# Gate groups of a product-key expert layer: 48 blocks with two groups each in place of 64 with one and a half, a column as the comparison's second scalar, and later first row gathers

## What is computed

```python
top_s, top_i = lax.top_k(s, 16)            # per head and half: 16 of 128 sub-keys
expert_idx, gates = ...                    # per token and head: 16 of 128 x 128 experts
def block_fn(args):
    xb, ib, gb = args
    u = jnp.take(expert_u, ib, axis=0)
    act = jax.nn.gelu(jnp.einsum('td,thkd->thk', xb, u).astype(jnp.float32))
    w = (gb * act).astype(xb.dtype)
    v = jnp.take(expert_v, ib, axis=0)
    return jnp.einsum('thk,thkd->td', w, v)
```

## Time and profile before

| | before |
|---|---|
| median of 3 runs | 4706.14 us (4703.5 to 4707.44) |
| the profiled execution: its own time | 4705.2 us |
| the profiled execution: its span | 4703.3 us |
| busy: TensorE, VectorE, ScalarE, GpSimd | 4041.3, 2219.0, 1623.2, 1626.7 us |
| granted TensorE clock, mean of the span | 0.885 |

### The profile page before, as it was taken

How to read it: one execution, slowest core, us unless ns; L and a number is a source line. 1 busy time by engine, 2 the same in 40 slices (tenths; PEclk the granted TensorE clock), 3 DMA queues, 4 the chain that set the end, 5 groups by cost and what they waited for, 6 DMA issues and landing times. The chain is left out here.

```text
span 4703.3 us, 53589 instructions
## 1 busy us (share of the span) xinstructions
PE 4041.3 (86%) x17473; PEld 3196.8 (68%) x17473; DVE 2219.0 (47%) x4053; ACT 1623.2 (35%) x2537; POOL 1626.7 (35%) x896
## 2 busy tenths in 40 slices
PE   6798768998769989998877979696989888889998
PEld 5437556876525458886765857575889888878886
DVE  1642172321233323302483141313788988768887
ACT  2322253322241133312353112322324666533334
POOL 3103234433200024433353422232468555543221
PEclk8759889998865579999988989897999999999999
DMA  2002102222100013222201312121366677899997
GB/s 87 28 8 82 60 19 76 97 91 68 47 15 1 0 48 104 89 80 80 69 1 54 95 52 72 58 85 65 125 214 227 220 260 266 277 360 359 343 344 250
DMA packets 275081, 573.60 MB, mean 122 GB/s; under 512 B 119777, under 2 KB 156001, under 8 KB 274545
## 3 DMA queue, kind: packets, MB, share of 16 engines
q1 hardware_dynamic: 238080, 437.71, 28.3%
q0 software_dynamic: 36864, 134.23, 8.4%
HBM read 517.33 MB, written 54.53 MB: 122 GB/s over the span
## 5 line engine op out<-in xcount | busy, mean ns | idle before, releaser
L382 PE MATMUL ps<-h_hi,w_hi 128*128 128x512 f32 (+1 forms) x3020 | 1155.7, 383 | 276.8 <-POOL w_lo L2158 95.4
L383 PE MATMUL ps<-h_lo,w_hi 128*128 128x512 f32 (+1 forms) x3020 | 1144.2, 379 | 0.0
L384 PE MATMUL ps<-h_hi,w_lo 128*128 128x512 f32 (+1 forms) x3020 | 1142.8, 378 | 0.0
L476 POOL TENSOR_TENSOR w_lo<-ring,w_hi 128x1024 fp32r<-128x1024 f32 (+3 forms) x193 | 463.3, 2401 | 1141.4 <-ACT w_hi L453 1141.4
L382 PEld LDWEIGHTS ps<-h_hi,w_hi 128*128 128x128 f32 x3020 | 585.2, 194 | 378.3 <-issue 146.2
L384 PEld LDWEIGHTS ps<-h_hi,w_lo 128*128 128x128 f32 x3020 | 584.1, 193 | 80.8
L383 PEld LDWEIGHTS ps<-h_lo,w_hi 128*128 128x128 f32 x3020 | 585.3, 194 | 78.4
L453 ACT CAST w_hi<-ring 128x1024 fp32r<-128x1024 f32 (+3 forms) x193 | 202.7, 1050 | 867.6 <-PE ps L384 808.3
L2158 POOL TENSOR_TENSOR w_lo<-ring,w_hi 128x1024 fp32r<-128x1024 f32 x142 | 363.0, 2560 | 336.3 <-ACT w_hi L2033 335.9
L2033 ACT CAST w_hi<-ring 128x1024 fp32r<-128x1024 f32 x270 | 281.9, 1044 | 383.6 <-PE ps L384 294.7
L382 PE MATMUL ps<-w_hi,one_hots 128*128 128x512 f32 x768 | 304.5, 396 | 4.1 <-DVE one_hots L2415 4.1
(11 more groups left out here) (358 smaller groups left out, 6969.6 us busy)
## 6 DMA issues: line engine op xcount, KB each, us to landing
ring<-in_expert_u SPq DMA_DIRECT2D x128, 512.0 KB, 4.1
ring<-in_expert_v SPq DMA_DIRECT2D x128, 512.0 KB, 5.6
ring<-in_w_gate_up SPq DMA_DIRECT2D x88, 512.0 KB, 3.7
acts<-expert_gelu SPq DMA_DIRECT2D x128, 192.0 KB, 1.9
gates<-peer_region SPq DMA_DIRECT2D x48, 512.0 KB, 3.1
peer_region<-acts SPq DMA_DIRECT2D x128, 192.0 KB, 4.6
peer_region<-gates SPq DMA_DIRECT2D x128, 192.0 KB, 5.6
ring<-in_w_down SPq DMA_DIRECT2D x32, 704.0 KB, 4.1
```

Source lines behind the costliest of these rows:

```text
L382: pe.matmul(out, w_hi, x_hi, start=start, stop=False)
L383: pe.matmul(out, w_hi, x_lo, start=False, stop=False)
L384: return pe.matmul(out, w_lo, x_hi, start=False, stop=stop)
L476: pool.tensor_tensor(half(c.w_lo, s), raw(s), half(c.w_hi, s).bitcast(F32), ALU.subtract).then_inc(c.lo_done.sem, 1)
```

## The change

Four edits. (1) `GATED` is 48 and each of these blocks has two groups, 2b and 2b + 1; the 24 blocks behind them are plain (8 before). (2) `rows_by`: the first four gathers stand behind `low` of block 14 in place of 8, the further early ones are spread over the blocks from there to 56, and in the gated blocks there are two gathers behind each `low`. Behind the `low` of block 56 + b the gathers asked so far are 26 + 2b (from b = 3 on); before, 28 + 1.5b rounded down. (3) SyncE stores up to two pieces of the gate table per block, in the plain blocks too, where before it stored one per block and all those left at once behind the last gated block. (4) The comparison L2401 takes a column of ones from SBUF as its second scalar in place of the constant 1.0, as L2402 beside it takes the gate's column.

```diff
-GATED = 64
-TAIL = 4
+GATED = 48
+GATHER_AT = 14
@@
 def groups_of(b):
-    return range((3 * b + 1) // 2, (3 * b + 4) // 2)
+    return range(2 * b, 2 * b + 2)

 def rows_by(n):
-    if n < 8:
+    if n < GATHER_AT:
         return 0
     if n < PLAIN:
-        return 4 + (n - 8) * EARLY_DOTS // (PLAIN - 8)
-    return min(P, 4 + EARLY_DOTS + max(0, (3 * (n - PLAIN - 4) + 6) // 2))
+        return 4 + (n - GATHER_AT) * EARLY_DOTS // (PLAIN - GATHER_AT)
+    return min(P, 4 + EARLY_DOTS + max(0, 2 * (n - PLAIN - 4) + 3))
@@ SyncE
-                    for h, e in waiting[0:1]:
+                    for h, e in waiting[0:2]:
                         keep_gates(h, e)
-                    waiting = waiting[1:]
+                    waiting = waiting[2:]
@@
-                for h, e in waiting:
-                    keep_gates(h, e)
                 for n in range(PLAIN + GATED, LAST):
                     up(n + 4, n % 4)
                     keep_act(n, n % 4)
+                    for h, e in waiting[0:2]:
+                        keep_gates(h, e)
+                    waiting = waiting[2:]
@@ VectorE
-                        dve.tensor_scalar(hots[:, 0, g % 3, s, :], iota[:], IJG[:, 0, t], 1.0, ALU.is_equal, ALU.mult)
+                        dve.tensor_scalar(hots[:, 0, g % 3, s, :], iota[:], IJG[:, 0, t], c.ones[:, 0:1], ALU.is_equal, ALU.mult)
```

## The result

| | before | changed |
|---|---|---|
| median | 4706.79 us (4 runs beside the changed kernel: 4703.5 to 4707.44, and one of 7889.4) | 4904.65 us (4 runs, 4902.18 to 4906.15) |
| profiled execution: own time, span | 4705.2, 4703.3 | 4906.15, 4904.2 |
| granted TensorE clock, mean | 0.885 | 0.868 |

The ratio of the fast runs, which leaves the one of 7889.4 us out, is 1.0422, 95% interval 1.041 to 1.0435: the changed kernel is 4.2% slower. The forecast was 4912 us, between 4862 and 4962.

What follows compares the result with a forecast made beforehand. It took the loop of late-asked rows in the gated blocks as the bound. Stage +224.8 us, first gathers -18, V blocks unchanged: +206.8 on the profiled 4705.2 gave 4912 us, range 4862 to 4962.

Steps and rivals of the forecast that it cites:

- Rows are asked late, and the loop now carries two groups: In the gated blocks, low parts, `high`, `low`, gather, dot and one-hots form a loop, carrying two groups per turn, not three.
- The round: One turn of the loop in the gated blocks, from low parts to low parts: 13.5 us, 44 of them.
- VectorE's wait for rows: VectorE's total wait for gathered rows, claimed to grow from 56 us to about 207 us or more.
- The gather 5.2: Landing time of a gather in the loop, 5.2 us, a little above the median of 5.1 because of stores ahead.
- The stage: From TensorE's arrival at block 56 to the first V block: 511.7 us before, 736.5 after, so +224.8.
- The tail's 3 for transfers: Added for transfers in the plain blocks behind the gated ones: 3 us, bounds 0 and 10.
- the burst of stores: Eight stores at once behind the gated blocks and TensorE's 10.17 us behind them, claimed to be gone after the change.
- The first gathers, 18: First gathers moved from block 8 to block 14: 18 us gained before block 56, between 10.9 and 20.2.
- The column, 0.24 on the loop and no end to the holds: L2401's second column: 0.06 us per start, 0.24 per round; L2401 still held while GpSimd makes `low`.
- (A): Rival: rows no wait, nothing held; gated blocks at VectorE's pace, 6.4 us each; about 4600 us; 4 in 100.
- (B): Rival: rows no wait but holds remain; gated blocks 8.8 us each; no change, 4705 us; 3 in 100.
- (C): Rival: TensorE, its clock falling, joins the loop; round some 15.3 us, +79, about 4990 us; 5 in 100.

## Why the prediction was right

By its own steps:

- *Rows are asked late, and the loop now carries two groups.* Right, and shown: the chain has the predicted links, and moving the gathers by two rows took 214 us away. The round was put at 13.5 and is 13.36 on average. VectorE's wait for rows was put at 207 us and is 204.6.
- *The gather 5.2.* Right as a mean (5.1 over the rounds), of two kinds: 4.1 to 4.6 with no stores and 5.9 to 6.7 with two.
- *The stage.* 736.5 forecast, 728.7 measured. Of the 7.8 us less, 6.5 had come by the last one-hots (622.0 behind the arrival at block 56, forecast 622.9 + 5.6), which is the 0.14 per round. The tail's 3 for transfers was near: one wait of 2.38. The gain that the prediction saw in the burst of stores gone is real with 48 blocks, but what the spread stores saved behind the loop (11.5 us) they cost within it (12.3 from group 5's one-hots to the last).
- *The first gathers, 18.* The changed kernel's profile gained 16.5, inside the forecast's 10.9 to 20.2. Alone in the kernel before, the edit was worth 21.6, just above that range, though its interval (13 to 26 us) doesn't tell the two apart. The profiles of the kernels with late gathers reach block 56 between 3608 and 3616 us, 16.5 to 24 us earlier, with the same first gathers in all; what makes them differ is open, so that 16.5 came out inside the range is in part luck.
- *The column, 0.24 on the loop and no end to the holds.* Right in kind; 12.7 us by the test where the sum had 10.6. By the Trainium skill (VectorE: DVE Perf Modes, section Mode 2×_2P) an instruction with one tensor source, in SBUF, can use both read ports. The holds agree and are the same in number with either form, but the price is not: a second column took 0.06 us more in each test. Whether this comes from fetching it or from a slower mode no run here tells.
- *Rivals.* (A) and (B), rows no wait, are what the kernel becomes with rows two earlier: 4690.8, where (B) had 4705. (A) asked for holds to end as well, and they don't. (C), TensorE in the loop: its clock fell to 0.76, but it waited 201.6 us for one-hots, so it had time to spare. Its busy share was 66%, where under 60% was expected with the proviso of a low clock.

## What to carry to other kernels

When work of one kind is dealt out behind work of another (here rows behind blocks), write the lead down as a loop: which instruction's end allows the request, which one needs it, and how many units one turn advances. The price of the loop is per turn, so a schedule that packs more into fewer blocks gets slower if a turn carries less, whatever the engines' busy shares say; one constant was worth 214 us here. Before adding an operand so that an engine is no longer held by another, look whether the trace already has that form next to the other engine's instruction: in the kernel before five instructions of it showed that it is held too.

## What the hardware showed that was not expected

- A comparison with two columns is held by GpSimd's subtraction as the one with a column and a constant is. In the changed kernel it was held even when by the profile it started 0.01 us ahead of `low` (3899.98 for 2.52 us, `low` at 3899.99); 16 of the 47 started 0.00 to 0.09 us ahead.

```profile
3899.73 0.35 DVE L2402 TENSOR_SCALAR one_hots<-iota,chosen_turned,basic 128x128 fp32r<-128x128 f32 x1
3899.98 2.52 DVE L2403 TENSOR_SCALAR one_hots<-iota,chosen_turned,gate_hi 128x128 fp32r<-128x128 f32 x1
```

- Two stores of 512 KB issued within 2 us ahead of a gather of 512 KB put its landing from 4.4 to 6.0 us, 0.8 each; with one store, in the kernel with the old stores, the median is 5.2.
- A longer instruction on VectorE (0.06 us) cost more than its own length in the kernel before, 14 us in place of at most 7, because it also moved the two engines against each other: the hold on the path grew from 1.79 to 2.09 us, 9 us over 30 rounds.
